# A two-block hybrid transformer kernel: another order for the weight preparation and the half sums around the two MLPs, and another assignment of buffers in the second merge

## The reference

```python
# layer 1: three branches (S5, short convolution, forgetting attention)
proj = einsum('bld,dn->bln', rmsnorm(x, g_pre_mix), w_in)
merged = sum over 3 branches of sigmoid(gate_i) * (y_i @ w_branch_i)
x = x + rmsnorm(merged @ w_out, g_post_mix)
ff = square(relu(rmsnorm(x, g_pre_mlp) @ w_ff1)) @ w_ff2        # 1024 -> 4096 -> 1024
x = x + rmsnorm(ff, g_post_mlp)
...
# layer 2: four branches (banded attention, HGRN, spatial gating, RG-LRU)
merged = sum over 4 branches of sigmoid(gate_i) * (o_i @ w_branch_i)
x = x + rms_norm(merged @ w_out, norm_mix_post)
gt, up = split(rms_norm(x, norm_ffn_pre) @ w1, 2)
x = x + rms_norm((silu(gt) * up) @ w2, norm_ffn_post)           # 1024 -> 2816 -> 1024
```

## Time and profile before

| what | value |
|---|---|
| median of 3 runs | 3335.32 us (3334.18 to 3335.87) |
| the profiled execution | 3335.87 us |
| its span, first to last instruction | 3334.5 us |
| PE busy | 3215.8 us (96%), 15473 matmuls |
| DVE busy | 1915.4 us (57%), 2449 instructions |
| ACT busy | 1247.5 us (37%) |
| POOL busy | 1044.8 us (31%) |
| mean granted clock of PE | 0.992 |

### The profile page before, as it was taken

How to read it: one execution, slowest core, us unless ns; L and a number is a source line. 1 busy time by engine, 2 the same in 40 slices (tenths; PEclk the granted TensorE clock), 3 DMA queues, 4 the chain that set the end, 5 groups by cost and what they waited for, 6 DMA issues and landing times.

```text
span 3334.5 us, 40301 instructions
## 1 busy us (share of the span) xinstructions
PE 3215.8 (96%) x15473; PEld 2605.8 (78%) x15473; DVE 1915.4 (57%) x2449; ACT 1247.5 (37%) x1855; POOL 1044.8 (31%) x618
## 2 busy tenths in 40 slices
PE   8999999999999999899999999999999999999997
PEld 6788777877886788777768788787778678888776
DVE  6752455444318887766653336572463587777666
ACT  3212444344325434443433333312343443334343
POOL 2111222222342222444622124341245222223445
PEclk9999999999999999999999999999999999999998
DMA  3544434325422545444424223214254223234434
GB/s 134 165 104 146 132 134 140 125 77 205 136 95 103 196 162 208 178 141 152 162 102 145 93 76 133 83 64 157 79 207 177 77 101 119 109 111 173 158 133 152
DMA packets 140906, 445.30 MB, mean 134 GB/s; under 512 B 14944, under 2 KB 24544, under 8 KB 137120
## 3 DMA queue, kind: packets, MB, share of 16 engines
q1 hardware_dynamic: 139680, 439.11, 37.8%
q10 hardware_dynamic: 1040, 3.67, 0.3%
HBM read 303.59 MB, written 142.15 MB: 134 GB/s over the span
## 4 chain that ended last, share of the span: by engine, by line
PE 51%; DVE 9%; issue 2%; ACT 2%; DMA 2%; POOL 1%; SPq 0%; DVEq 0%; ACTq 0%; POOLq 0%
PE pair L2253 25%; PE pair L332 19%; PE pair L451 3%; DMA w_raw<-in_stream 1%; DVE f1hl L2456 1%; DVE wide L2102 1%; DVE bank L2100 1%; PE bank L662 1%; PE wide L842 1%; POOL w_lo L2123 0%; PE bank L810 0%; DVE f2hl L2456 0%; PE wide L575 0%; PE wide L1521 0%; DVE act_lo L565 0%
## 5 line engine op out<-in xcount | busy, mean ns | idle before, releaser
L293 POOL TENSOR_TENSOR w_lo<-w_raw,w_hi 128x1024 fp32r<-128x1024 f32 (+1 forms) x184 | 392.6, 2141 | 1366.8 <-ACT w_hi L289 1326.1
L332 PE MATMUL pair<-act_hi,w_hi 128*128 128x512 f32 x1888 | 609.3, 404 | 4.0 <-DVE p L2584 1.5
L332 PE MATMUL pair<-act_lo,w_hi 128*128 128x512 f32 x1888 | 585.5, 391 | 0.0
L332 PE MATMUL pair<-act_hi,w_lo 128*128 128x512 f32 x1888 | 583.9, 391 | 0.0
L332 PEld LDWEIGHTS pair<-act_hi,w_lo 128*128 128x128 f32 x1888 | 355.1, 188 | 77.1
L332 PEld LDWEIGHTS pair<-act_lo,w_hi 128*128 128x128 f32 x1888 | 355.1, 188 | 76.8
L332 PEld LDWEIGHTS pair<-act_hi,w_hi 128*128 128x128 f32 x1888 | 334.5, 189 | 67.3 <-issue 10.2
L633 DVE TENSOR_TENSOR p<-pair,rs 128x1024 f32<-128x1024 f32 x100 | 122.3, 1223 | 391.4 <-PE pair L332 391.3
L289 ACT CAST w_hi<-w_raw 128x1024 fp32r<-128x1024 f32 x154 | 161.9, 1051 | 477.8 <-PE pair L332 424.1
L2123 POOL TENSOR_TENSOR w_lo<-w_raw,w_hi 128x512 fp32r<-128x512 f32 (+1 forms) x120 | 189.9, 1592 | 187.8 <-ACT w_hi L2116 187.8
L2253 PE MATMUL pair<-act_hi,w_hi 128*128 128x512 f32 x474 | 184.5, 389 | 0.0
(11 more groups left out here) (653 smaller groups left out, 6692.7 us busy)
## 6 DMA issues: line engine op xcount, KB each, us to landing
w_raw<-in_stream SPq DMA_DIRECT2D x275, 512.0 KB, 3.8
proj<-p SPq DMA_DIRECT2D x101, 512.0 KB, 2.6
act_lo<-hidden SPq DMA_DIRECT2D x42, 512.0 KB, 4.9
sums<-f1y SPq DMA_DIRECT2D x16, 1024.0 KB, 4.1
m2g<-proj SPq DMA_DIRECT2D x32, 512.0 KB, 5.5
sums<-f2y SPq DMA_DIRECT2D x11, 1024.0 KB, 4.1
hidden<-f1y SPq DMA_DIRECT2D x21, 512.0 KB, 3.5
hidden<-f2y SPq DMA_DIRECT2D x20, 512.0 KB, 2.6
```

What stands on the lines that cost most here:

```text
L293: last = nc.gpsimd.tensor_tensor(wlo[:, slot, at:at + n], raw[:, slot, at:at + n], whi[:, slot, at:at + n].bitcast(F32), ALU.subtract)
L332: last = nc.tensor.matmul(out_pair[:, h * HALF:(h + 1) * HALF], wt, a[:, h * HALF:(h + 1) * HALF], start=k == 0 and n_pass == 0, stop=k == ...
```

## The change

Six places are edited; the operations, their sizes and their number stay the same.

1. Second merge: sum and part buffers are exchanged, so the first sum goes to `buf[:, 0]`, and the wait for the stored rows stands ahead of block 0 for both merges.
2. `weights_at`: `w_sum(q, 1)` and `w_high(q, 1)` both stand in the slot of p = 6, for step 1 too. `w_low(q, 1)` comes ahead of the sums 4 and 2 in the slot of p = 2.
3. Ahead of the loop: the four T2 low parts and the high and low part of weight combination 4 move ahead of T1's casts and of the second eviction.
4. `fourth_sums` moves from the slot of (0,2) to that of (0,1), and `w_high(1, 0)`, `w_low(1, 0)` are taken out of it.
5. Step 1's weights are prepared in the slots of the same p as in all other steps; its slot-6 part follows `fourth_sums` in the slot of (0,1).
6. `finish` of the last inner step but one (q = pairs - 1 in the loop) moves from the slot of p = 4 to that of p = 3, two products earlier. Only for q = pairs it stays at p = 4.

```diff
--- before.py
+++ after.py
@@ -1847,7 +1847,7 @@
         def evict(i, o, psum, ready, read):
             block, br = o // branches, o % branches
             part, g, m = parts[br % 2], gates[br], sums[block % len(sums)]
-            if o == (2 if branches == 4 else 0):
+            if o == 0:
                 V.after(*rows_stored())
             if br == 0:
                 done = read(V.then(ready, opened[o]).tensor_tensor(m, g, psum[:], ALU.mult))
@@ -2138,13 +2138,11 @@
                 w_high(q, 0)
                 w_low(q, 0)
                 w_sum(q, 1)
+                w_high(q, 1)
             elif p == 2:
-                if q == 1:
-                    w_sum(q, 1)
-                w_high(q, 1)
+                w_low(q, 1)
                 w_sum(q, 4)
                 w_sum(q, 2)
-                w_low(q, 1)
             elif p == 3:
                 w_high(q, 2)
                 w_high(q, 3)
@@ -2185,17 +2183,17 @@
         w_sum(0, 6)
         for _ in range(KT):
             next(second)
+        for k in range(4):
+            t_low(T2, k, high[T2, k])
         w_high(0, 3)
         w_low(0, 3)
+        w_high(0, 4)
+        w_low(0, 4)
         for k in range(4):
             high[T1, k] = t_high(T1, k)
         for _ in second:
             pass
         advance(2, 2)
-        for k in range(4):
-            t_low(T2, k, high[T2, k])
-        w_high(0, 4)
-        w_low(0, 4)
         for k in range(4):
             t_low(T1, k, high[T1, k])
         w_high(0, 5)
@@ -2212,9 +2210,6 @@
                 high[T4, k] = t_high(T4, k)
                 if k:
                     t_low(T4, k - 1, high[T4, k - 1])
-                if k == 2:
-                    w_high(1, 0)
-                    w_low(1, 0)
             t_low(T4, 3, high[T4, 3])
             w_low(0, 6)
 
@@ -2478,7 +2473,7 @@
                 if (n, p) == (last, 6):
                     split_unit(after + 1, 1 - after % 2, (after + 1) // 2 + 1)
                 (inner if n < pairs else outer)(n, p)
-                if q == 0 and p == 2:
+                if q == 0 and p == 1:
                     fourth_sums()
                 if q and p == 0:
                     w_low(q, 4)
@@ -2494,7 +2489,7 @@
                     split_role(changing, 0 if p == 3 else 1)
                 if opened is not None and (n - q, p) in split_late:
                     split_role(opened, split_late[n - q, p], done[q - 1, 5])
-                if 0 < q <= pairs and p == (4 if q >= pairs - 1 else 3):
+                if 0 < q <= pairs and p == (4 if q == pairs else 3):
                     finish(q - 1)
                 if q + 2 in next_group and p in (0, 1):
                     load_early(next_group[q + 2], 4 + p)
@@ -2505,11 +2500,11 @@
                         split_role(opened_last, 7)
                 if q == pairs and p == 2:
                     G.mark(G.after(V.last(), A.last()).memset(squares[:], 0.0))
-                if q == 0:
-                    for step in {3: (2,), 4: (3,), 5: (5, 4)}.get(p, ()):
-                        weights_at(1, step)
-                elif q < last:
-                    weights_at(q + 1, p)
+                if q < last:
+                    if n == q or q:
+                        weights_at(q + 1, p)
+                    if q == 0 and p == 1:
+                        weights_at(1, 6)
                 elif n == last:
                     if len(roles[p]) == 1:
                         SP.wait_ge(*done[last, p])
@@ -2664,7 +2659,7 @@
             w.again(78)
             gmlp_lru(ops, stored, freed)
             gates2, sum2 = sb(at, "m2g", [P, 4, L]), sb(at, "m2s", [P, L])
-            merging = merge(ops, proj2, GATE2, 4, None, [gates2[:, n, :] for n in range(4)], [sum2[:], buf[:, 0, :]], [buf[:, 1, :], rs[:]],
+            merging = merge(ops, proj2, GATE2, 4, None, [gates2[:, n, :] for n in range(4)], [buf[:, 0, :], sum2[:]], [rs[:], buf[:, 1, :]],
                             [(V.last(), A.last()), (), (), [s.last() for s in outs]], lambda: [s.last() for s in outs], {})
             next(merging)
         advance(52, 52)
```

## The result

| | before | after |
|---|---|---|
| median of 4 runs each, same chip | 3334.75 us (3331.67 to 3335.87) | 3354.41 us (3351.94 to 3358.98) |
| ratio | 1 | 1.006, 95% interval 1.0048 to 1.0074 |
| profiled execution, and its span | 3335.87, 3334.5 us | 3352.41, 3351.1 us |
| mean granted clock of TensorE | 0.992 | 0.992 |

The change costs 0.6%, 19.7 us between the medians and 16.6 between the profiled spans. The other 3 us lie within the scatter of single runs, some 3 us either way. The forecast was 3360, in a range of 3344 to 3371, so the time lies inside it. But two of the terms were wrong in sign, so the total says less than the places do.

A forecast was written before the change was run, and what follows sets the result against it. TensorE alone was taken to bound the bulk of each MLP, but not the starts and inner-to-outer change-overs. Terms summing to 25.3 us on 3335.87 gave 3361.2, or 3360.6 against the median; predicted 3360, range 3344 to 3371.

The forecast's parts named there:

- (a): Rival: reordering at starts, change-overs and boundaries costs about half, moved operations finding POOL between its operations; 3348 us; chance 0.15.
- Second merge, +4.3: Second merge: first eviction waits for both output rows, starting 5.04 us later; less a swallowed 0.75 us gap, +4.3 us.
- Start of the first MLP, +3.0: First MLP's start: (0,4) stalls 3.8 us for its seed, (1,1) comes 4.2 later, 1.2 recovered from later DVE waits; +3.0 us.
- Start of the second MLP, +3.4: Second MLP's start: the seed of (0,4) comes late, (1,1) starts at 2719.2 against 2715.8, no later gaps to recover; +3.4 us.
- Inner to outer, first MLP, +5.2: First MLP's change-over: earlier finish takes turns with POOL, delaying splits 3.4 us; new cast order adds 0.9 twice; +5.2 us.
- Inner to outer, second MLP, +3.3: Second MLP's change-over: finish is one multiply, so less delay; 1.5 left at T4 plus 0.9 twice; +3.3 us.
- the T3 split ends at 3080.3: Step at the second MLP's change-over: with finish moved earlier, the T3 split ends at 3080.3, the T2 split at 3088.5.
- Clock, +3.6: TensorE's granted clock: three new long idles, at the merge and (0,4) of each start, cost 1.2 us each; +3.6 us.
- Group boundaries, 5 x 0.5: Later group boundaries, three and two: second w_sum held by POOL costs 0.5 us at the next product, +2.5 us together.
- Steady state, 0: Steady periods: the seed delayed 0.6 us and w_high(2) 0.7, both hidden by TensorE; zero.
- (b): Rival: all reordering is hidden or given back, only the second merge's wait shows; 3339.6 us, within 0.2%; chance 0.10.
- (c): Rival: faster, as DVE no longer waits for ACT's cast before w_low(q+1,1) and gaps set by DVE go; 3323; chance 0.07.

The follow-up runs named there:

- the order alone: Kernel before, with only the order inside `weights_at` changed for steps from 2 on: w_high(q,1) in slot 6, w_low(q,1) ahead of two sums; 3337.39 us, ratio 0.9999.
- the starts alone: Kernel before, with only edits 3, 4 and 5, and the new order of `weights_at` only for step 1; 3343.13 us, ratio 1.0018.

## Why the prediction was right, and where not

**The total.** The forecast for the profiled execution was 3361.2, and it took 3352.4, 8.8 less. Two places make 7.8 of that, the inner to outer of the second MLP (-0.4, 3.3 forecast) and the boundaries of the first (-2.6, 1.5 forecast). The measured median lies 5.6 us below the forecast and 6.4 above rival (a), so the total alone does not choose between them; the places do. Both errors point downward, so the range held by its width and not because the terms were right.

**Second merge, +4.3:** right. The eviction is released by the landing of proj<-p. The merge alone cost 5.6 in its trace, 4.4 without the slow matmuls behind the wait; the whole change has 5.1, where 5.5 were forecast with the clock.

**Start of the first MLP, +3.0:** right in its steps. (0,4) waited 3.30 where 3.8 was forecast, (1,1) started at 1101.37 where 1100.95 was, and among what the line L2248 waits for in the trace after d_read does not appear, where the earlier trace rows has 5.2 us of it. The part came to 3.9, of which 1.7 were lost to slow matmuls between (0,4) and (1,0), where the clock term had 1.2; what was summed to 3.0 is thus 2.2. Moving only the slot-6 part behind the seed gave back 3.6 us here and 4.7 in the second MLP.

**Start of the second MLP, +3.4:** right, 4.4 with 1.7 of slow matmuls; (0,4) waited 4.05, between the term and its upper bound of 4.5.

**Inner to outer, first MLP, +5.2:** right, 4.6. The turns of DVE and POOL were the step that mattered, and shrinking two of POOL's operations took 4.1 of the 4.9 us away. The wait was 4.56 and not 5.3: I had the four sums end at 1349.3, and they ended at 1351.73, which is 1348.6 once the 3.1 us are taken off by which all was late there. The lock that the Trainium skill states, page "SBUF — State Buffer", section "SBUF: two separate sides", agrees with these rows, 1.63 to 2.90 us against 0.68. That the move gains without it is shown in part, by the 1.1 us that the run with two of POOL's operations shrunk ended ahead of before.

**Inner to outer, second MLP, +3.3:** wrong in sign, -0.4. The failed step is "the T3 split ends at 3080.3". I had kept DVE and POOL in the order of before, POOL first, at 3071.06, and cost `finish` by itself. But edit 2 puts w_low(20,1) ahead of w_sum(20,4) on DVE, so that DVE, which had been held there (1.68 us for a sum at 3067.82 before), reached the first split 0.5 us earlier against TensorE (3085.05 less the 14.2 us by which everything was late, against 3071.35), and before POOL did. The T3 split then ended at 3091.85, which is 3077.7 without those 14.2 us, and the T2 split at 3083.2 instead of 3088.5. With `finish` alone, DVE kept its 3.21 us turn and the place cost 1.2. With the order alone DVE came first too, but the multiply still stood ahead of the T2 split, (20,2) waited 1.91 us (2.04 before), and the place cost 2.0, 1.8 of it forecast. Each edit was costed rightly alone, and their meeting was not looked at.

**Group boundaries, 5 x 0.5:** the mechanism was right, one wait in three pieces and about 0.1 us longer, and in the order alone they came out the same. The sizes were wrong in both MLPs, for two reasons. In the first, -2.6, they were set by the clock: behind the first boundary it no longer fell (0.50 to 1.00), at the second it did (1.00 to 0.72). The merge alone has 2.1 there, without an edit at the boundaries, so this figure is not owed to the change for certain. In the second, +2.6, no matmul was slow behind either boundary, before or after. Its first boundary added the 0.5 forecast; the other 2.1 arise in the last group, where the order alone has the same. Its products take 2.04 us instead of 2.72 and can hide less of the work between them; that this is the reason is argued, not tested. The failed step is the equal price for all five boundaries.

**Clock, +3.6:** the three new dips came, by the count of spacings 2.2 us in the merge and 1.4 and 1.6 behind the two (0,4), but others went, and the sum is 1.6 us in 29.6. The step that failed was to count the new waits and leave the old ones as they were.

**Steady state, 0:** right. Between (3,1) and (13,0) of the first MLP no wait appeared that was not there before. In the second, 0.6 us came back over the steps up to 19, 0.07 in every other one, and the same with the order alone.

**Rivals.** (b), that only the merge shows, falls with the starts alone and `finish` alone, each slower. (c), faster, falls with ACT's row at 1090.31: w_high(1,1) was done at 1090.9, not by 1088.9. (a), in which the moved operations find POOL between its own, falls in the first MLP with the four sums at 1.63 to 2.90 us; in the second the change-over cost even less than it says.

## What to carry to other kernels

Before an operation is moved up in an in-order queue, list what now stands behind it and which engine waits for that: one cast of 0.58 us, put ahead of a copy, held TensorE for 3.30 and 4.05 us, because its own input came from the end of another engine's chain. Where two engines take turns, cost the edits together, for an edit elsewhere that brings one of them 0.5 us forward can exchange who goes first, and with that the sign of a term. And look at what stands ahead of the work that TensorE waits for at each opening: putting the next step's preparation behind it gave 0.35%, more than any other edit tried here.

## What was not expected of the hardware

Turns cost the side that comes second up to a whole operation of the other, with operands in SBUF: a 128x512 operation of DVE took 0.68 us alone and up to 2.90, one of 128x1024 1.21 to 3.44, and POOL's 128x1024 2.41 to 3.30. A DVE operation with one input in PSUM was not held: d_read (L2310) took 0.68 us at 1342.07, while POOL's operation of 1341.01 ran.

The granted clock did not follow the length of the last wait alone: after 3.44 us it was 0.50 at one boundary and 1.00 at the next, and after 2.50, 0.52 and 0.52 us it was 1.00 at the first and 0.72 behind the same three waits at the second. A single wait of 2.04 us was enough for 0.52 from 3087 to 3090. What decides between them, no run here settles.
